# Another order of the first loads and of VectorE's first work in a two-block transformer kernel on one Trainium2 core

## The reference

```python
cond = jax.nn.silu(c)
mod = (cond @ ada_w[layer] + ada_b[layer])[:, None, :]
sh1, sc1, g1, sh2, sc2, g2 = jnp.split(mod, 6, axis=-1)
h = rms_norm(x, norm_mix_g[layer]) * (1.0 + sc1) + sh1
x = x + g1 * hybrid_mixer(h, positions, w_in[layer], ...)
```

## Time and profile before

| | |
|---|---|
| median of 3 runs (lowest, highest) | 3293.91 us (3282.50, 3302.66) |
| span of the profiled execution | 3284.7 us |
| PE busy | 3056.3 us, 93% |
| DVE busy | 2001.9 us, 61% |
| ACT busy | 1234.2 us, 38% |
| mean granted TensorE clock | 0.956 of 2.4 GHz |
| read from HBM | 508.31 MB |

### The profile page before, as it was taken

The page is one execution under the profiler, slowest core; times in us unless marked ns, Lnnn a source line. Parts: engine busy times, 40 slices in busy tenths (PEclk is TensorE's granted clock), DMA queues, the critical chain, the costliest instruction groups (busy, mean ns, idle before and its releaser), DMA issues.

```text
span 3284.7 us, 48802 instructions
## 1 busy us (share of the span) xinstructions
PE 3056.3 (93%) x18248; PEld 2642.3 (80%) x18248; DVE 2001.9 (61%) x2670; ACT 1234.2 (38%) x1488; POOL 118.3 (4%) x227
## 2 busy tenths in 40 slices
PE   3879999789999999989999999999999999977999
PEld 2758998579999999987888777788877878763899
DVE  6746677556666666666757535565656656544555
ACT  2225444244454544444232322422224222421543
POOL 0100001000000000000000000000000000000000
PEclk9879999789999999999999999999999999977999
DMA  7805777026665665653535232343433444210354
GB/s 265 310 26 167 249 252 282 25 95 211 207 211 191 202 206 199 203 185 118 190 130 174 101 103 93 106 155 126 160 133 125 155 133 155 64 46 0 117 192 162
DMA packets 118712, 511.03 MB, mean 156 GB/s; under 512 B 12848, under 2 KB 16304, under 8 KB 118336
## 3 DMA queue, kind: packets, MB, share of 16 engines
q1 hardware_dynamic: 83936, 381.99, 34.6%
q0 software_dynamic: 32112, 117.45, 10.7%
q10 hardware_dynamic: 2544, 9.96, 0.8%
HBM read 508.31 MB, written 1.05 MB: 155 GB/s over the span
## 4 chain that ended last, share of the span: by engine, by line
PE 86%; DVE 7%; ACT 3%; DMA 2%; issue 2%; ACTq 0%; DVEq 0%; POOLq 0%
PE PS L1279 26%; PE PS L1281 26%; PE PS L1280 26%; DMA ada<-in_adastream 2%; DVE PS L715 1%; PE PS L1290 1%; DVE stage_b L707 1%; PE PS L1638 1%; PE PS L1637 1%; ACT h_hi L456 1%; PE PS L1302 1%; PE PS L1467 1%; PE PS L1306 1%; PE PS L1475 1%; ACT stage_b L456 1%
## 5 line engine op out<-in xcount | busy, mean ns | idle before, releaser
L1279 PE MATMUL PS<-h_hi,whi 128*128 128x256 f32 (+1 forms) x3904 | 1250.0, 320 | 30.1 <-DVE wlo L694 15.6
L1280 PE MATMUL PS<-h_lo,whi 128*128 128x256 f32 (+1 forms) x3904 | 1244.2, 319 | 0.0
L1281 PE MATMUL PS<-h_hi,wlo 128*128 128x256 f32 (+1 forms) x3904 | 1244.0, 319 | 0.0
L421 ACT ACTIVATE whi<-raw 128x1408 fp32r<-128x1408 f32 (+1 forms) x556 | 725.8, 1313 | 822.9 <-PE PS L1281 751.9
L694 DVE TENSOR_TENSOR wlo<-raw,whi 128x1408 fp32r<-128x1408 f32 (+1 forms) x556 | 842.6, 1540 | 276.3 <-ACT whi L421 275.9
L1279 PEld LDWEIGHTS PS<-h_hi,whi 128*128 128x128 f32 x3904 | 739.5, 189 | 100.2 <-issue 24.5
L1280 PEld LDWEIGHTS PS<-h_lo,whi 128*128 128x128 f32 x3904 | 739.2, 189 | 59.8 <-issue 2.0
L1281 PEld LDWEIGHTS PS<-h_hi,wlo 128*128 128x128 f32 x3904 | 738.8, 189 | 58.1
L1279 PE MATMUL PS<-hid_hi,whi 128*128 128x256 f32 (+1 forms) x1584 | 504.8, 319 | 0.0
L1281 PE MATMUL PS<-hid_hi,wlo 128*128 128x256 f32 (+1 forms) x1584 | 504.8, 319 | 0.0
L1280 PE MATMUL PS<-hid_lo,whi 128*128 128x256 f32 (+1 forms) x1584 | 504.8, 319 | 0.0
(11 more groups left out here) (279 smaller groups left out, 1826.6 us busy)
## 6 DMA issues: line engine op xcount, KB each, us to landing
raw<-in_wstream SPq DMA_DIRECT2D x436, 704.0 KB, 5.0
ada<-in_adastream POOLq DMA_DIRECT2D x222, 512.0 KB, 4.5
raw<-in_wstream SPq DMA_DIRECT2D x120, 512.0 KB, 4.4
ada_first<-in_adastream ACTq DMA_DIRECT2D x6, 1536.0 KB, 24.0
con<-in_consts SPq DMA_DIRECT2D x1, 1031.5 KB, 17.7
X<-in_xT SPq DMA_DIRECT2D x1, 1024.0 KB, 13.5
X<-in_ctxT SPq DMA_DIRECT2D x1, 1024.0 KB, 5.7
cond<-in_c_rows POOLq DMA_DIRECT2D x1, 1024.0 KB, 9.7
```

Source lines behind the costliest of these rows:

```text
L421: nc.scalar.activation(whi[:, q % SLOTS, 0:n], raw[:, q % SLOTS, 0:n], ACT.Copy).then_inc(hi_split, 1)
L1279: mm(o, left[0], right[0], start=start, stop=False)
L1280: mm(o, left[0], right[1], start=False, stop=False)
L1281: return mm(o, left[1], right[0], start=False, stop=stop)
```

## The change

- **Loads.** SP issues positions, the first 257 columns of the constants (identity, ones and the frequencies, which are moved forward in the table), cond, X and vec; then waits until the fourth ada_first transfer (tiles 10 to 13) has landed instead of the second; then the four panels, and only then the small weights and the other 1806 columns of constants, on a semaphore `const_in`; then the context. ACT's queue no longer carries cond. It loads ada_first in five transfers (2, 4, 4, 4, 4 tiles) from a second copy of the 18 tiles in which a partition's tiles lie one behind the other, so a row is 8 KB in the first and 16 KB in the other four. POOL waits for the last of them, not the fourth of six.
- **DVE.** It first waits for `early_in` at 48 (positions, constants' head, vec), does the angles, then products 0 to 5, the additions of squares, products 6 to 9, norm 0's reciprocal root (`inverse`, cut out of `norm`), products 10 to 15, mods1, split_lo of panel 0, and enters norm 0 at the spread root. split_lo of panels 1 and 2 stands inside the norm's loop, products 16 and 17 behind it after a wait for `const_in` at 64, and after them the mixer.
- **ACT.** Sine and absolute value, then cond's Silu, the other sine, the squares, the root, split_hi of panel 0; split_hi of panels 1 and 2 inside the norm.
- **PE.** No stay_warm in norm 0; it waits for `const_in` behind first_tiles.

```diff
+FIRST_LOADS = ((0, 2), (2, 4), (6, 4), (10, 4), (14, 4))
...
+            sp.dma_start(posi.bitcast(I32), pos).then_inc(early_in, 16)
+            sp.dma_start(con[:, 0:EARLY], consts[:, 0:EARLY]).then_inc(early_in, 16)
+            sp.dma_start(cond[:, 0, :], c_rows[:, 0, :]).then_inc(cond_in, 16)
             sp.dma_start(X[:, :, 0:SEQ], xT).then_inc(x_in, 16)
-            sp.dma_start(vec[:, :], vecs).then_inc(small_in, 16)
...
+            sp.dma_start(vec[:, :], vecs).then_inc(early_in, 16)
+            sp.wait_ge(ada_first_in[3], 16)
...
-            pool.wait_ge(ada_first_in[3], 16)
+            pool.wait_ge(ada_first_in[4], 16)
...
                     ins.then_inc(h_hi_ready, 1)
+                    if n == 0 and c in (1, 3):
+                        split_hi(c // 2 + 1)
...
+            for j, (t, n) in enumerate(FIRST_LOADS):
+                act.dma_start(ada_first[:, t:t + n, :], ada0[:, t:t + n, :]).then_inc(ada_first_in[j], 16)
             act.wait_ge(S("angle_reduced"), 1)
             nc.scalar.activation(trig[:, 1, :], red, ACT.Sin)
             nc.scalar.activation(turns, red, ACT.Abs).then_inc(S("angle_abs"), 1)
+            act.wait_ge(cond_in, 16)
+            nc.scalar.activation(cond[:, 0, :], cond[:, 0, :], ACT.Silu).then_inc(cond_ready, 1)
             act.wait_ge(S("angle_cos"), 1)
             nc.scalar.activation(trig[:, 0, :], angle, ACT.Sin).then_inc(S("trig_ready"), 1)
-            for q in range(AHEAD):
-                split_hi(q)
+            act.wait_ge(x_in, 16)
+            squares(SEQ, 0)
+            roots(0)
+            split_hi(0)
...
+                    if n == 0 and c in (2, 4):
+                        split_lo(c // 2)
...
-            for g in range(1, KD // 2):
-                add_squares(SEQ, g, 0)
+            dve.wait_ge(early_in, 48)
+            angles()
             dve.wait_ge(cond_ready, 1)
-            for t in range(ADA_FIRST):
...
+            for t in range(2 * KD):
...
+                if t == 6:
+                    for g in range(1, KD // 2):
+                        add_squares(SEQ, g, 0)
+                if t == 10:
+                    inverse(0)
                 modulation(t, ada_first[:, t, :], [mod1[:, 0, t:t + 1]], t, bank=0)
...
             mods1(0, (0,), 0, 2 * KD)
+            split_lo(0)
...
+                    if l == 0:
+                        dve.wait_ge(const_in, 64)
+                        for t in range(2 * KD, ADA_FIRST):
+                            modulation(t, ada_first[:, t, :], [mod1[:, 0, t:t + 1]], t)
                     mixer(l)
...
-                if n != FINAL1:
+                if n and n != FINAL1:
                     stay_warm(bank, 2 + T // BOTH)
...
+                pe.wait_ge(const_in, 64)
...
+    ada0 = np.ascontiguousarray(adastream[0:ADA_FIRST].transpose(1, 0, 2))
```

More of the change, by code:

```diff
@@ L111, in constants @@
     out = {"ident": np.eye(PART), "ones": np.ones((PART, PART))}
+    half = RET_DK // 2
+    inv = 10000.0 ** (-np.arange(half) / half)
+    out["inv_freq"] = np.concatenate([inv, inv])[:, None]
     out["causal"] = same & (t[None, :] >= t[:, None])
@@ L153 @@
 CONSTS = _c
+EARLY = CONST["inv_freq"][0] + CONST["inv_freq"][1]
 TWO_PI = 2.0 * np.pi
@@ L160, with build @@
 PI_MAX = float(np.nextafter(np.float32(np.pi), np.float32(0)))
-def build(nc, wstream, adastream, c_rows, vecs, consts, xT, ctxT, pos, w_ga, w_alpha, router, out, last="end"):
+def build(nc, wstream, adastream, ada0, c_rows, vecs, consts, xT, ctxT, pos, w_ga, w_alpha, router, out, last="end"):
     ctx = ExitStack()
@@ L281, in build @@
         posi, angle, turns, red = (angles_in[:, i, :] for i in range(4))
-        x_in, ctx_in, small_in, pos_in = sem("x_in"), sem("ctx_in"), sem("small_in"), sem("pos_in")
+        x_in, ctx_in, early_in, const_in = sem("x_in"), sem("ctx_in"), sem("early_in"), sem("const_in")
         raw_in = [sem(f"raw_in{i}") for i in range(SLOTS)]
@@ L288, in build @@
         panel_used = sem("panel_used")
-        ada_first_in = [sem(f"ada_first_in{i}") for i in range(6)]
+        ada_first_in = [sem(f"ada_first_in{i}") for i in range(len(FIRST_LOADS))]
         ada_done = sem("ada_done")
@@ L722, in ring_tile, with inverse @@
                 modulation(t, ada[:, r % ADA_SLOTS, :], cols, first, di)
-            def norm(n):
-                T = NORMS[n][0]
-                w = T // PART
+            def inverse(n):
+                w = NORMS[n][0] // PART
                 dve.wait_ge(sumsq_ready, n + 1)
@@ L732, in norm @@
                 spread(diag[:, 0:w, :], rstd[:, 0:w], w).then_inc(diag_ready, 1)
+            def norm(n):
+                T = NORMS[n][0]
+                if n:
+                    inverse(n)
                 dve.wait_ge(bc_ready, n + 1)
@@ L1182, in _ @@
             nc.vector.memset(zc0[:, 1:2], 0.0).then_inc(evacuated, 1)
[L1183 to L1184 removed]
+            dve.wait_ge(early_in, 48)
+            angles()
             dve.wait_ge(cond_ready, 1)
[L1186 to L1194 removed]
+            for t in range(2 * KD):
+                if t in [first for first, _ in FIRST_LOADS]:
+                    dve.wait_ge(ada_first_in[[first for first, _ in FIRST_LOADS].index(t)], 16)
+                if t == 6:
[3 more added lines that the diff above has]
+                    inverse(0)
+                modulation(t, ada_first[:, t, :], [mod1[:, 0, t:t + 1]], t, bank=0)
             mods1(0, (0,), 0, 2 * KD)
+            split_lo(0)
             for l, ff in enumerate(("dense", "moe")):
@@ L1285, in weights, with stay_warm @@
                 return whi[:, q % SLOTS, w], wlo[:, q % SLOTS, w]
-            def stay_warm(bank, count):
+            def stay_warm(bank, count, rhs=C("ret_decay")):
                 for _ in range(count):
-                    mm(PS[:, bank, :], ones, C("ret_decay"), start=True, stop=True)
+                    mm(PS[:, bank, :], ones, rhs, start=True, stop=True)
             def norm(n):
```

27 lines of the change are left out of this document (8 added, 19 removed).

## The result

| | before | after |
|---|---|---|
| median of 20 runs (lowest, highest) | 3292.81 us (3280.62, 3302.66) | 3304.78 us (3289.36, 3314.85) |
| ratio after to before | | 1.0030, 95% interval 1.0019 to 1.0042 |
| span of the profiled execution | 3284.7 us | 3312.4 us |

The change costs 9.9 us by the ratio (6 to 14), 12.0 by the medians; 14.7 was forecast.

A forecast was written before the change was run, and what follows sets the result against it. The prediction took the kernel as bound by TensorE, but its first 73 us by a DVE string; 7.9 us up to norm 0 plus 6.8 to the first ring product made +14.7, so 3308.6 us, range 3287 to 3320.

The forecast's parts named there:

- The queues take turns by rows: Loads at the start: engines take one row from each queue in turn, whatever its length, so vec lands at 31 us.
- rival 2: Loads at the start: long rows are cut to 4 KB; vec lands at 24.1, +7.8 us, 3301.7 us; chance 0.13.
- T: DVE's entry into norm 0's eight tiles: 56.95 us before, forecast at 64.9, 7.9 later.
- From the input to the norm: DVE's start: first product 6.2 us after vec lands, then 27.7 us of back-to-back work up to norm 0.
- E: Time when vec, the last input DVE first waits for, lands: about 31 us, bounds 12.8 and 31.
- The norm and the wait for panel 3: Norm 0 to first ring product: longer loop, PE idle 4.4 us, then 24 matmuls at half clock, 5.1 us.
- The term +6.8: Norm 0's entry to first ring product: 6.8 us more than 15.94; at full clock 4.3 more.
- Sum: Whole kernel: 7.9 + 6.8 = +14.7 us, added to the median of 3293.9, gives 3308.6 us.
- The prediction's own sign for a start that does not carry through: Whole kernel: if all marks are right but time is not up by 10 us or more, carrying through fails.
- Rival 3: Mixer: its waits for ring and panels absorb the late start, leaving 3294 us; chance 0.09.
- Rival 1: Loads at the start: queues share by bytes, DVE starts at 12.8 us, kernel gains 3.5, 3290 us; chance 0.13.
- The balance ahead of T: Check on DVE's string before norm 0: 17.5 us added, 10.5 leaving (products, splits, angles, broadcast wait), net 7.0.

The follow-up runs named there:

- made by hand: Changed kernel with ACT's five ada_first transfers reading the first copy again, so that rows are 4 KB: ratio to before 1.0028 (1.0009 to 1.0047).
- with the input at 10.0 us, by other means: Changed kernel with vec ahead of cond and X, 4 KB rows, products 16 and 17 behind the splits, additions and root later: ratio to before 0.9975.
- second profile: The changed kernel, nothing altered, profiled once more: span 3306.6 us, first mixer copy at 84.71 us.
- with PE warm: Changed kernel with six unread matmuls of 256 columns on PE behind the 14th product, ahead of the projection: span 3301.4 us, copy at 84.83 us.
- vec first: Changed kernel with SP issuing vec ahead of cond and X: ratio to before 1.0003 (0.9988 to 1.0018).

## Why the prediction was right, point by point

- **The queues take turns by rows.** Right, and the time of the first input rests on it. vec was put at 31 us; DVE's cast is at 31.63. X lands at 31.1 (2.26 + 28.8). The rule that engines go round queue rows packet by packet (the Trainium skill, DMA: Bandwidth & Descriptors, "Queues, rings and completion order") agrees with the turns, with one row here as a packet: from 9.0 to 9.7 us the 16 engines took 17 rows of one queue and 16 of the other. The preferred packet of 4096 bytes ("SWDGE vs HWDGE vs iDMA" in the same page of the Trainium skill, in a table on the descriptors that GpSimd builds) was no limit here, where ACT issued the transfers: 47 rows carried 0.77 MB, 16 KB each. So rival 2 falls, and its price was right where its case was made by hand: 25.7 us for 24.1, T 58.8 for 58.0.
- **From the input to the norm.** 6.2 us to the first product was forecast, 6.21 measured (37.84 - 31.63); T 64.9, measured 64.74. That T is met so closely is in part luck: the input came 0.6 us later than E, and the string from the first product to T took 26.9 us and not 27.7, mostly as its 16 products took 21.0 for 21.6. The second table load is there, 1.28 us on the path.
- **The norm and the wait for panel 3.** The term +6.8 was too large: measured 84.46 - 64.74 - 15.94 = +3.8, and in the second profile +5.1. Two parts were mis-sized. The loop with its two splits took 12.2 us (64.74 to 76.96), not 13.1, and the split of panel 3 was done at T + 15.9, not 17.0. And PE's idle stretch was taken at 4.4 us and the clock at half for all 24 matmuls, 5.1 us; it was 2.47 us at a granted clock of 1.00 and 3.1 us, or 3.61 at 0.50 and 4.4 us. In the first profile PE was not through its sixth tile at T + 12.6 but at T + 13.5 (80.70 - 2.47 is T + 13.49), and this shortened the wait as well; in the second it was through at T + 12.3. At full clock the prediction had +4.3, and the profile at full clock gives 3.8. That a slow start of PE is hidden by the wait holds too: with PE warm it only waited longer.
- **Sum.** +14.7 forecast; +11.6 and +12.4 us at the first ring product, +9.9 (6 to 14) by the ratio. 3308.6 us against 3304.78. The term +6.8 was 3.0 us too large in one profile and 1.7 in the other, and what the ring product is late agrees with the times of the whole. The prediction's own sign for a start that does not carry through, less than 10 us, is just touched by the ratio and not by the medians (12.0); the interval covers the 11.6 us of the ring product, so it doesn't speak against it.
- **Rival 3, absorbed.** Fallen: in the kernel before, 28 us of delay gave 27 to 39.
- **Rival 1, sharing by bytes.** Fallen by the rows. That a start at 12.8 us would gain remains true in kind: with the input at 10.0 us, by other means, the kernel gained.
- **A share of what is lost is in the norm.** The balance ahead of T counted two products and two splits as leaving the string; they are only moved behind T. With vec first T is 5.5 us earlier and the copy only 0.6.

## What to carry to other kernels

When two queues are full, count rows, not bytes: in this kernel, merging one queue's rows into longer ones took bandwidth from the other in proportion. Put a small transfer on which the first instruction waits ahead of everything large in its own queue, and give large rows only to transfers that nothing competes with. And compare a mark just behind the changed place before comparing spans: here 12 us of the difference between two profiles came from a stretch of which no instruction was changed.

## What was not expected of the hardware

PE being faster ahead of a wait went with a lower clock behind it: in the first profile it was idle 2.47 us, kept a granted clock of 1.00 and reached the copy 19.1 us after T; in the second, and in the run with warming, it was idle 3.61 and 3.65 us, fell to 0.50 and needed 20.4 and 20.5. SP's issue of a small transfer took 9.98 us (vec, five transfers deep, behind X's 1024 rows), where it took 0.64 before; SP had only a wait until 23.6 us to come behind it, so nothing in the trace is late for that. In the profile of after the windows from 66 to 72 us read a granted clock of 1.00, while the matmuls there stood 0.21 us apart, the pitch of 0.50 in the earlier trace rows, until 72.6 us: this column doesn't show such a slow start, and the number of matmuls does. And the same mixture of experts took from 775.9 to 787.9 us, at 838 or 828 matmuls in 98 us of a PE that was never idle and was granted full clock.
